# A mixture-of-experts layer that gathers its token rows by a slot table, instead of scattering them to HBM first

## The reference

```
h = modulated rms_norm(x)                       # per column: gain and shift
group = argmax of 4 group logits; 2 best of its 4 experts, weighted by a softmax
y[token] = sum over the 2 chosen experts of weight * (silu(h W1[e]) * (h W3[e])) W2[e]
x = x + gate_row * y
```

## Time and profile before

| | us |
|---|---|
| median of 3 runs (3838.61 to 3840.31) | 3839.18 |
| the profiled execution's own time | 3840.37 |
| its span, first to last instruction | 3838.6 |
| PE busy | 3356.0 (87%) |
| DVE busy | 2047.6 (53%) |
| ACT busy | 1328.2 (35%) |
| POOL busy | 220.4 (6%) |

### The profile page before, as it was taken

How to read it: one execution, slowest core, us unless ns; L and a number is a source line. 1 busy time by engine, 2 the same in 40 slices (tenths; PEclk the granted TensorE clock), 3 DMA queues, 4 the chain that set the end, 5 groups by cost and what they waited for, 6 DMA issues and landing times. The chain is left out here.

```text
span 3838.6 us, 39125 instructions
## 1 busy us (share of the span) xinstructions
PE 3356.0 (87%) x15102; PEld 2590.3 (67%) x15102; DVE 2047.6 (53%) x2698; ACT 1328.2 (35%) x1710; POOL 220.4 (6%) x241
## 2 busy tenths in 40 slices
PE   2999998899989999888999797885995987685995
PEld 2888765788878887567888585464884454544884
DVE  2555415455445544255554544545886256735886
ACT  2322215222222222243222324623884121313884
POOL 0000000000000000000000003422001000012001
PEclk9999898999999999989999897987997999886998
DMA  8333231333223323304331411025995211025995
GB/s 273 139 148 113 89 109 33 126 148 135 84 110 148 148 88 113 111 1 159 148 131 55 153 33 67 1 103 220 413 414 214 94 44 44 23 80 212 416 415 216
DMA packets 89600, 553.78 MB, mean 144 GB/s; under 512 B 9376, under 2 KB 10272, under 8 KB 41200
## 3 DMA queue, kind: packets, MB, share of 16 engines
q1 hardware_dynamic: 71760, 485.76, 32.8%
q0 software_dynamic: 13088, 49.29, 3.6%
q10 hardware_dynamic: 4608, 16.78, 1.1%
HBM read 524.49 MB, written 48.28 MB: 149 GB/s over the span
## 5 line engine op out<-in xcount | busy, mean ns | idle before, releaser
L211 PE MATMUL ffn_gate_up<-ffn_h_high,ffn_gate_up_high 128*128 128x512 f32 x1408 | 548.3, 389 | 7.1 <-DVE ffn_h_low L245 7.1
L213 PE MATMUL ffn_gate_up<-ffn_h_high,ffn_gate_up_low 128*128 128x512 f32 x1408 | 548.0, 389 | 0.0
L212 PE MATMUL ffn_gate_up<-ffn_h_low,ffn_gate_up_high 128*128 128x512 f32 x1408 | 547.8, 389 | 0.0
L2244 DVE TENSOR_TENSOR moe_low<-moe_raw,moe_high 128x2048 fp32r<-128x2048 f32 x192 | 433.7, 2286 | 38.9 <-ACT moe_high L2151 38.6
L454 ACT ACTIVATE ffn_silu_gate<-ffn_gate_up 128x512 f32<-128x512 f32 x88 | 52.7, 598 | 970.2 <-PE ffn_gate_up L213 970.2
L2151 ACT ACTIVATE moe_high<-moe_raw 128x2048 fp32r<-128x2048 f32 x192 | 364.2, 1917 | 19.4 <-PE moe_bank L213 19.4
L485 DVE TENSOR_TENSOR ffn_product<-ffn_silu_gate,ffn_gate_up 128x512 f32<-128x512 f32 x88 | 60.5, 687 | 564.4 <-ACT ffn_silu_gate L454 564.4
L211 PEld LDWEIGHTS ffn_gate_up<-ffn_h_high,ffn_gate_up_high 128*128 128x128 f32 x1408 | 264.3, 188 | 63.2 <-DVE ffn_h_low L245 8.4
L213 PEld LDWEIGHTS ffn_gate_up<-ffn_h_high,ffn_gate_up_low 128*128 128x128 f32 x1408 | 264.3, 188 | 55.1
L212 PEld LDWEIGHTS ffn_gate_up<-ffn_h_low,ffn_gate_up_high 128*128 128x128 f32 x1408 | 264.3, 188 | 55.0
L211 PE MATMUL ffn_down<-ffn_down_high,ffn_hid_high 128*128 128x512 f32 x704 | 282.7, 402 | 2.5 <-DVE x_tok L509 2.4
(11 more groups left out here) (488 smaller groups left out, 5700.9 us busy)
## 6 DMA issues: line engine op xcount, KB each, us to landing
moe_raw<-in_moe_w SPq DMA_DIRECT2D x192, 1024.0 KB, 8.0
ffn_raw_gate_up<-in_ffn_gate_up SPq DMA_DIRECT2D x88, 1024.0 KB, 6.7
ffn_ada_w<-in_ada_w SPq DMA_DIRECT2D x32, 1536.0 KB, 6.7
ffn_raw_down<-in_ffn_down SPq DMA_DIRECT2D x88, 512.0 KB, 3.3
mixer_w_raw<-in_mix_w SPq DMA_DIRECT2D x24, 1024.0 KB, 5.4
hgrn_ring<-in_hgrn_w SPq DMA_DIRECT2D x10, 2048.0 KB, 7.6
moe_xe<-moe_rows POOLq DMA_DIRECT2D x32, 512.0 KB, 9.4
moe_y<-moe_y ACTq DMA_DIRECT2D x32, 512.0 KB, 9.1
```

The source lines that it names most:

```text
L211: pe.matmul(out, lhsT[0], rhs[0], start=first, stop=False)
L212: pe.matmul(out, lhsT[0], rhs[1], start=False, stop=False)
L213: return pe.matmul(out, lhsT[1], rhs[0], start=False, stop=last)
L2244: dve.tensor_tensor(low[n % SPLITS][:, :, :], raw[n % RAWS][:, :, :], high[n % SPLITS][:, :, :].bitcast(FP32), ALU.subtract)\
```

## The change

- `start` writes no zeros. `moe_rows` is gone; the last 896 rows of `moe_y` are zeroed in `moe_0` by one DMA that POOL issues after the logits.
- The token rows come from TensorE: 32 transposes turn `hT` back, ACT copies them to `h_tok`, and SP stores them to a new tensor `moe_tok` (512 rows in token order) between the seventh and the eighth weight chunk.
- A table `token_in` (for each slot and expert the token's number) is made on TensorE: DVE compares each pair's rank with the slot numbers (`in_slot`, 128x1024), and eight matmuls with `token_hot` add up the token numbers. In unused slots the sum is 0, which is the number of token 0. POOL then gathers each expert's rows from `moe_tok` with an indirect DMA.
- Logit matmuls stand between the transposes; they go to four banks. Gain and shift rows are gone; the gate row's diagonal comes from ACT. The counts take 8 matmuls, not 14. DVE issues alike small instructions without a wait between them (`later`, `settle`), splits chunks 0 and 1 inside the table's work, and makes slots and weights after it.
- The overflow block has POOL in it, and DVE waits there for the last output store before it reads the count.
- In the combine block DVE, not POOL, adds to x.

```diff
@@ start
-            for rows in (chip.dram["moe_rows"], chip.dram["moe_y"][NE * P:SLOT_ROWS, :]):
-                pool.dma_start(rows.rearrange("(r p) d -> p r d", p=P),
-                               chip.dram["moe_zeros"].unsqueeze(1).broadcast_to([P, rows.shape[0] // P, DM])).then_inc(chip.rows_zeroed, 16)
@@ moe, sync
+                if n == RAWS:
+                    for t in range(TT):
+                        sp.wait_ge(h_tok_ready, 2 * t + 2)
+                        sp.dma_start(dram["moe_tok"][P * t:P * t + P, :], h_tok[:, t, :]).then_inc(tok_stored, 16)
@@ moe, tensor
+            for o in range(8):
+                if o >= 4:
+                    pe.wait_ge(h_tok_ready, o - 3)
+                for k in range(4):
+                    last = pe.transpose(ps[o % 4][:, k * P:(k + 1) * P], norm.hT[:, 4 * (o % 2) + k, (o // 2) * P:(o // 2 + 1) * P],
+                                        chip.ident[:, :])
+                last.then_inc(h_turned, 1)
...
+            pe.wait_ge(in_slot_ready, 1)
+            for i in range(2 * TT):
+                last = pe.matmul(ps[5][:, 0:NE], in_slot[:, i, :], token_hot[:, i // TT, i % TT, :], start=(i == 0), stop=(i == 2 * TT - 1))
+            last.then_inc(token_in_done, 1)
+            pe.wait_ge(row_ready, 2)
+            pe.wait_ge(token_in_ready, 1)
@@ moe, scalar
+            for o in range(8):
+                act.wait_ge(h_turned, o + 1)
+                act.activation(h_tok[:, o // 2, 512 * (o % 2):512 * (o % 2) + 512], ps[o % 4][:, :], ACT.Copy).then_inc(h_tok_ready, 1)
+            for k in range(KT):
+                ins = act.activation(gate_row[:, k * P:(k + 1) * P], chip.ident[:, :], ACT.Copy, scale=mod[:, 2, k:k + 1])
+            ins.then_inc(diag_ready, 1)
@@ moe, gpsimd
-            pool.wait_ge(scattered, 16 * 2 * TT)
+            if layer == 0:
+                pool.wait_ge(logits_done, 1)
+                unused = dram["moe_y"][NE * P:SLOT_ROWS, :].rearrange("(r p) d -> p r d", p=P)
+                pool.dma_start(unused, dram["moe_zeros"].unsqueeze(1).broadcast_to([P, NOV, DM])).then_inc(chip.rows_zeroed, 16)
+            pool.wait_ge(tok_stored, 16 * TT)
+            pool.wait_ge(token_in_ready, 1)
             for e in range(NE):
                 if e >= 2:
                     pool.wait_ge(x_turned, e - 1)
-                pool.dma_start(xe[e % 2][:, :], dram["moe_rows"][P * e:P * e + P, :]).then_inc(xe_loaded[e % 2], 16)
+                pool.indirect_dma_start(xe[e % 2][:, :], None, dram["moe_tok"],
+                                        bass.IndirectOffsetOnAxis(token_in[:, e:e + 1], 0)).then_inc(xe_loaded[e % 2], 16)
@@ moe, vector
+            own(dve.reduce_sum(rank_of[:, :, :], route[:, :, :, :], AXX))
+            dve.tensor_tensor(in_slot[:, :, :], slot_no.unsqueeze(1).broadcast_to([P, 2 * TT, P]),
+                              rank_of[:, :, :].rearrange("p a t -> p (a t)").unsqueeze(2).broadcast_to([P, 2 * TT, P]),
+                              ALU.is_equal).then_inc(in_slot_ready, 1)
             own(dve.tensor_scalar(over[:, 1, :], count, float(P), None, ALU.is_gt))
+            dve.wait_ge(token_in_done, 1)
+            dve.tensor_copy(token_in[:, :], ps[5][:, 0:NE]).then_inc(token_in_ready, 1)
+            make_low(1)
@@ moe, overflow, vector
+            dve.wait_ge(y_stored[1], 16 * (NE // 2))
             with if_overflow(dve):
```

More of the change, by code:

```diff
@@ L2094, in _ @@
[L2094 to L2095 removed]
+            pe.wait_ge(small_loaded, 32)
+            for k in range(KT + 3):
+                if k < KT:
+                    if k >= 4:
+                        norm.bank_free(pe, k - 4)
+                    for t in range(TT):
+                        if k == 0:
+                            if t == TT - 1:
+                                pe.wait_ge(norm.xn_ready[0], 1)
+                            else:
+                                pe.wait_ge(norm.xn_ready[1], t + 1)
+                        last = pe.transpose(ps[k % 4][:, t * P:(t + 1) * P], norm.xn[:, t, k * P:(k + 1) * P], chip.ident[:, :])
+                    last.then_inc(norm.turned, 1)
+                if k >= 3:
+                    pe.wait_ge(norm.hT_ready[(k - 3) % 2], (k - 3) // 2 + 1)
+                    for t in range(TT):
+                        last = pe.matmul(ps[4 + t][:, 0:20], norm.hT[:, k - 3, t * P:(t + 1) * P], w_router[:, k - 3, :],
+                                         start=(k == 3), stop=(k == KT + 2))
@@ L2140, in _ @@
         def _(act):
-            def take_row(r, bank):
-                act.wait_ge(row_done, r + 1)
-                for half in range(2):
-                    act.activation(rows[r][:, 512 * half:512 * half + 512], ps[bank + half][:, :], ACT.Copy).then_inc(row_ready, 1)
             def make_high(n):
@@ L2185, in _ @@
             act.activation(tiny[:, 1, :], tiny[:, 0, :], ACT.Exp).then_inc(exp_out, 1)
-            take_row(2, 2)
-            make_high(1)
+            act.wait_ge(row_done, 1)
+            for half in range(2):
+                act.activation(gate_row[:, 512 * half:512 * half + 512], ps[6 + half][:, :], ACT.Copy).then_inc(row_ready, 1)
             make_high(2)
@@ L2271, in _ @@
             dve.wait_ge(logits_done, 1)
-            own(dve.tensor_copy(logits[:, :, :].rearrange("p t c -> p (t c)"), ps[0][:, 0:TT * (NEG + NE)]))
+            for t in range(TT - 1):
+                own.later(dve.tensor_copy(logits[:, t, :], ps[4 + t][:, 0:NEG + NE]))
+            own(dve.tensor_copy(logits[:, TT - 1, :], ps[7][:, 0:NEG + NE]))
+            dve.sem_inc(logits_read, 1)
             dve.wait_ge(small_loaded, 32)
@@ L2380, in _ @@
                 with pe.Fori(0, NOV) as j:
+                    pe.wait_ge(over_equal, j + 1)
+                    for i in range(2 * TT):
+                        last = pe.matmul(ps[7][:, 0:1], equal[:, i, :], token_no[:, i % TT:i % TT + 1], start=(i == 0), stop=(i == 2 * TT - 1))
+                    last.then_inc(over_in_done, 1)
                     pe.wait_ge(xe_arrived, 16 * (j + 1))
```

141 lines of the change are left out of this document (75 added, 66 removed).

## The result

The changed kernel takes 3736.43 us (median of 4 runs, 3731.61 to 3738.78), the kernel before beside it on the same chip 3839.74: a ratio of 0.9729, 95% interval 0.9712 to 0.9746. 3737 was forecast. The profiled execution's span is 3735.2 us against 3838.6, 103.4 less.

A forecast was written before the change was run, and what follows sets the result against it. Bounds: start held by POOL's zeros, a serial 80.3 us wait ahead of the experts, then TensorE, always busy. 3840.4 − 49.6 (start) − 48.8 (ahead of experts) − 3.6 (ends) = 3738.4 profiled, 3737 median; range 3716 to 3762.

The forecast's parts named there:

- Start, −49.6: Start stage: without POOL's zeros the FFN's first load goes out at 10.9 us instead of 60.5.
- Norm, −5.2: Head of each MoE layer: three DVE sums take 1.22 us, not 2.96, without POOL's spreading beside them; −5.2 us.
- Transposes and logits, +0.3: Ahead of the experts, each layer: TensorE's transposes and logits get 0.3 us longer.
- Logits to counts, −0.7: Each MoE layer: 12.4 us, not 13.1, as TensorE's queue with turned-back transposes and gate row hides DVE's saving.
- Counts, −2.7: Each MoE layer: 16 TensorE records and latency take 3.6 us, where the counts took 6.3.
- counts to request, −18.0: Each MoE layer, from counts to POOL's request for the first expert's rows: 7.1 us instead of 25.1.
- Request to rows, +1.9: Each MoE layer: the first gather takes 5.2 + 0.7 us beside DVE's split, a plain load 4.0; bounds +0.5 and +6.
- Stores of token rows hidden, narrowly in `moe_0`: Ahead of the first gather: the stores end before the table is ready at 22; if not, 1 to 2 us once.
- Experts, 0: Experts' stretch: sixteen gathers replace sixteen loads at no cost, as long as the DMAs stay as fast.
- Rival 1: Experts' gathers: unused slots read token 0 too often, lengthening the loop, 3881 us with x = 5; chance 0.08.
- End, −1.8: End of each MoE layer: barrier behind the last store costs 1.7 us, combine gains 3.5.
- Rival 3: Ahead of the experts: TensorE gets its upper level, 2.4 GHz, −8 to −10 us per layer, 3719; chance 0.08.

The follow-up runs named there:

- experiment 1: Kernel before the change, with the start stage's two fills with zeros asked for by ScalarE, not POOL: 3814.46 us, ratio 0.9936.
- experiment 2: Changed kernel, with one 11.8 MB fill of moe_y back on POOL in the start stage and none in moe_0: 3773.55 us in one run.
- experiment 8: Changed kernel, with three 128x1024 products on POOL at the head of each MoE stage, beside the norm: 3733.48 us in one run.
- Experiment 7: Changed kernel, with sixteen unused 128x128 matmuls on TensorE ahead of the transposes in each MoE stage: 3723.53 us, ratio 0.9691.
- experiment 5: Changed kernel, with TensorE's matmuls for the gate row moved from ahead of the counts to behind the table of tokens: 3724.96 us, ratio 0.9699.
- experiment 6: Changed kernel, with VectorE's subtraction for weight chunk 1 moved behind its slot arithmetic: 3736.24 us in one run.
- experiment 10: Changed kernel with the edits of experiments 5, 6 and 7, eight more unused matmuls, and x and columns asked for at once: 3707.64 us, ratio 0.9654.
- experiment 11: Kernel of experiment 10, with POOL asking for moe_y's zeros at the start of moe_0, not after the logits: 3709.65 us, ratio 0.9659.
- experiment 12: Kernel of experiment 11, with VectorE's wait for the last store dropped and its overflow comparison written to xe1: 3708.45 us, ratio 0.9656.
- experiment 3: Changed kernel, with the token table multiplied by zero, so every fetched row is token 0: 3731.63 us, ratio 0.9723.
- experiment 4: Changed kernel, with every expert fetching tokens 0 to 127, each once: 3736.42 us, ratio 0.9729.
- experiment 9: Changed kernel, with the combine block's four 128x1024 additions to x given back to POOL: 3741.54 us in one run.

## Why the prediction was right, and where it was not

- **Start, −49.6:** −49.3. x took 0.8 longer than taken, the columns 0.3 less. The mechanism is shown by experiments 1 and 2, from both sides.
- **Norm, −5.2:** −5.0, shown by experiment 8. That the sum carries all of it is not shown: in experiment 8 the later start came with an earlier clock.
- **Transposes and logits, +0.3:** wrong in size, +3.5 and +3.8. The prediction took 0.5 us off for waiting and added 0.8 for the matmuls on the gain and shift rows, "which kept TensorE at work before". Experiment 7 shows what as much empty work there is worth: 7.5 and 8.2 us in the two layers against the changed kernel's profile, which has the slowest value of the draw. No run puts the removed matmuls themselves back, and they did not make the clock certain: in the four stages of the two kernels that have them (before, experiment 1) transposes and logits took 16.0 to 19.9. That was the step to weigh: work that did nothing on the path bore on the clock of what came behind it.
- **Logits to counts, −0.7:** −0.4 in `moe_0`, −3.7 in `moe_1`, where the gate row ran at the upper level. (The terms given add up to 12.7, not 12.4; `moe_0` had 12.9.) That this TensorE queue hides VectorE's saving was right, and experiment 5 shows it to be worth 9 to 11 us.
- **Counts, −2.7, and counts to request, −18.0:** as worked out, 3.5 and 7.0 in `moe_0`. This, the largest part in each layer, is read from the two traces; no run puts the scatter back alone.
- **Request to rows, +1.9:** +3.3 and +3.4. That VectorE's split doubles the issue was right and taken from the earlier trace rows; experiment 6 shows that the split costs 2.7 to 3.2 in all, more than the 0.7 taken.
- **Stores of token rows hidden, narrowly in `moe_0`:** right for this kernel only. In experiments 5 and 10 to 12 they are what the first fetch waits for.
- **Experts, 0:** −2.1 and 0.0. Rival 1 fell by experiments 3 and 4. In all 14 profiles the stretch lies between 287.5 and 290.6. The windows over that of `moe_0`, before and after, show that TensorE was busy 1.9 us longer before on the same 1336 records, at a lower mean clock:

```profile
2645.50:2935.00 289.50, 287.20 (x1336) 237.74 (x1336) 248.33 (x156) 222.22 (x187) 6.87 (x13) 0.98 0.91 368
```
```profile
2574.20:2862.00 287.80, 285.30 (x1336) 236.34 (x1336) 248.50 (x156) 222.42 (x188) 21.73 (x13) 0.99 0.92 371
```

Most of that lies in the last expert. Where its down matmuls begin, after a short idle time of TensorE, the clock was at the lower level for 3.4 us before, and not in the changed kernel:

```profile
2927.70:2931.10 3.40, 3.20 (x8) 2.56 (x9) 0.09 (x1) 0.00 (x0) 0.00 (x0) 0.50 0.00 0
```
```profile
2853.00:2860.00 7.00, 4.71 (x22) 3.70 (x22) 1.38 (x2) 1.20 (x2) 0.00 (x0) 1.00 0.00 0
```

Over the 14 profiles, 8 of the 28 stretches have this spell and take 289.1 to 290.6 us, and the 20 without it take 287.5 to 288.4. Kernels with the scatter and kernels with the gather are in both groups, so the 2 us are a draw and no work of the change; what sets it is open.

- **End, −1.8:** −3.3 and −3.5. The barrier cost 1.1 and 1.2, not 1.7; the combine gave 3.7 and 4.0, not 3.5 (experiment 9); and from the last addition to the next stage's or the program's end another 0.7 went, with VectorE and not POOL adding last.

So −102.0 was forecast and −103.4 came, and the closeness is partly luck: ahead of the experts 5.5 us less were won than forecast over both layers, and the ends (3.1), the experts (2.1) and the unchanged stages (1.9) gave 7.1 back. Rival 3, the upper level ahead of the experts at −8 to −10 a layer, is no other mechanism but the other side of the same draw: experiment 3 had 50.7 us in `moe_0` where the changed kernel's profile had 60.8.

## What to carry to other kernels

A DMA that GpSimd asks for holds the end of its block until it lands, though nothing waits for its data; ask for such a one where its engine's block goes on long enough. Before work is taken from an idle TensorE, look at what runs behind it and at which clock; and once a serial chain is shortened, look in its engines' queues for work that it doesn't need: the gate row in TensorE's was worth 9 to 11 us.

## Not expected of the hardware

- GpSimd is held at the end of its block by its open DMAs, ScalarE is not (experiments 1, 2). ScalarE's queue took a request for 3.6 MB behind one of 11.8 MB only after 26.3 us.
- A lone fetch of 128 rows of 4 KB landed and was seen by TensorE 4.3 to 4.7 us after its request without VectorE beside it, 7.3 to 8.0 with its 2.29 us `tensor_tensor` (experiment 6 and the others). One came between, 6.1 us without the `tensor_tensor`, while the DMA engines were full of weight chunks (`moe_0` of experiment 5).
- In the experts' stretch a fetch's issue took 1.70 in the median where a plain load took 0.53, and nothing waited for it.
- 128 reads of one row of 4 KB went as fast as 128 rows (10.8 us among other traffic).
- In the last expert of a MoE layer, with the clock at the upper level since early in the first expert and TensorE just idle for two short times (0.84 and 1.46 us), the granted clock fell to 0.50 for 3.4 us in 8 of 28 stretches, which cost about 2 us each (before: 2927.7 to 2931.1).
